# Where a level's product, its operands and the weights' remaining parts stand in the forget-gate phase

## The reference

```python
for l in range(DEPTH):
    h = rms_norm(x, norm_g[l])
    proj = h @ w_in[l]
    q_a, k_a, v_a, q_h, f_h, i_h, q_m, z = jnp.split(proj, split_points, axis=-1)
    o_a = moba_attention(partial_rope(rms_norm(q_a)), partial_rope(rms_norm(k_a)), v_a)
    o_h = rms_norm(hgrn2_chunkwise(q_h, f_h, i_h, lb_all[l]), hgrn_o_norm[l])
    o_m = memory_attention(rms_norm(q_m), km, vm)
    y = jnp.concatenate([o_a, o_h, o_m], axis=-1) * jax.nn.silu(z)
    x = x + y @ w_out[l]
# inside hgrn2_chunkwise, with lb from the layer
log_f = jnp.logaddexp(jnp.log(lb), jnp.log1p(-lb) + jax.nn.log_sigmoid(fl))
kf = (1.0 - lb) * jax.nn.sigmoid(-fl)
A = jnp.cumsum(lfc, axis=2)
decay = jnp.exp(jnp.where(causal[:, :, None], A[:, :, :, None, :] - A[:, :, None, :, :], -jnp.inf))
scores = jnp.einsum('bhtd,bhtsd,bhsd->bhts', qc, decay, kc)
```

## Time and profile before

| | |
|---|---|
| median of 3 runs | 1388.79 us |
| the profiled execution's own time | 1389.63 us |
| its span | 1387.8 us |
| TensorE matmul busy | 1349.3 us (97%) |
| VectorE busy | 971.3 us (70%) |
| ScalarE busy | 742.3 us (53%) |
| mean granted TensorE clock | 0.997 |

### The profile page before, as it was taken

One profiled execution on the slowest core, in us unless ns is written; L12 is line 12 of the kernel. 1 busy time (PEld: TensorE's weight loads), 2 busy tenths in 40 slices (PEclk: granted clock), 3 DMA queues, 4 the chain that ended last, 5 costly groups with the idle time before them and its releaser, 6 DMA issues.

```text
span 1387.8 us, 17865 instructions
## 1 busy us (share of the span) xinstructions
PE 1349.3 (97%) x7119; PEld 1146.4 (83%) x7119; DVE 971.3 (70%) x1230; ACT 742.3 (53%) x1045; POOL 57.0 (4%) x46
## 2 busy tenths in 40 slices
PE   7999999989999999999999999999999999999998
PEld 6978888978887898887877888879888887788886
DVE  6689776699776498747876555457796678565644
ACT  6864766764684565544454444346744444454432
POOL 1002000001100001000000000000100000000000
PEclk9999999999999999999999999999999999999999
DMA  8554335544343655434445554455643344476553
GB/s 294 186 169 155 100 122 182 183 129 155 113 144 131 224 176 174 147 126 144 152 152 182 182 182 168 166 180 185 200 157 123 120 143 146 145 221 186 189 180 110
DMA packets 139697, 226.25 MB, mean 163 GB/s; under 512 B 8096, under 2 KB 54880, under 8 KB 139488
## 3 DMA queue, kind: packets, MB, share of 16 engines
q1 hardware_dynamic: 137952, 222.49, 48.8%
q10 hardware_dynamic: 1664, 2.63, 0.5%
HBM read 224.05 MB, written 1.05 MB: 162 GB/s over the span
## 4 chain that ended last, share of the span: by engine, by line
PE 80%; DVE 12%; ACT 4%; issue 2%; POOL 1%; DMA 0%; SPq 0%; ACTq 0%; DVEq 0%
PE gp L613 61%; PE gp L602 7%; PE mp L585 4%; DVE arena L1466 4%; DVE wt_rest L1472 3%; PE mp L896 2%; PE mp L715 1%; DVE arena L1472 1%; PE mp L782 1%; DVE arena L1956 1%; POOL rs_out L2222 1%; DVE arena L1469 1%; PE mp L757 1%; ACT arena L1048 1%; PE mp L743 0%
## 5 line engine op out<-in xcount | busy, mean ns | idle before, releaser
L1472 DVE TENSOR_TENSOR wt_rest<-wt,wt_hi 128x1024 fp32r<-128x1024 f32 x156 | 184.1, 1221 | 77.6 <-ACT wt_hi L1080 76.9
L1080 ACT ACTIVATE wt_hi<-wt 128x1024 fp32r<-128x1024 f32 x156 | 156.8, 1054 | 101.9 <-DMA wt<-in_ffn_up 51.0
L1080 ACT ACTIVATE mix_hi<-wt 128x1024 fp32r<-128x1024 f32 x136 | 139.7, 1062 | 103.3 <-PE gp L613 58.4
L1472 DVE TENSOR_TENSOR wt_rest<-wt,mix_hi 128x1024 fp32r<-128x1024 f32 x136 | 160.5, 1220 | 34.2 <-ACT mix_hi L1080 33.3
L613 PE MATMUL gp<-wt_rest,mix_hT_hi 128*128 128x512 f32 x384 | 149.8, 390 | 0.0
L613 PE MATMUL gp<-mix_hi,mix_hT_hi 128*128 128x512 f32 x352 | 140.7, 400 | 4.6 <-DVE wt_rest L1472 3.7
L613 PE MATMUL gp<-wt_hi,hT_hi 128*128 128x512 f32 x352 | 140.2, 398 | 4.8 <-DVE wt_rest L1472 4.0
L613 PE MATMUL gp<-wt_hi,hT_rest 128*128 128x512 f32 x352 | 137.5, 391 | 0.0
L613 PE MATMUL gp<-mix_hi,mix_hT_rest 128*128 128x512 f32 x352 | 137.3, 390 | 0.0
L613 PE MATMUL gp<-wt_rest,hT_hi 128*128 128x512 f32 x352 | 137.2, 390 | 0.0
L1080 ACT ACTIVATE first_hi<-wt 128x1024 fp32r<-128x1024 f32 x104 | 106.4, 1061 | 49.1 <-PE gp L613 36.7
(11 more groups left out here) (331 smaller groups left out, 2913.7 us busy)
## 6 DMA issues: line engine op xcount, KB each, us to landing
wt<-in_w_in SPq DMA_DIRECT2D x100, 1024.0 KB, 5.0
wt<-in_ffn_gate SPq DMA_DIRECT2D x44, 512.0 KB, 4.0
wt<-in_ffn_up SPq DMA_DIRECT2D x44, 512.0 KB, 5.0
wt<-in_w_out SPq DMA_DIRECT2D x20, 1024.0 KB, 5.0
wt<-in_ffn_down SPq DMA_DIRECT2D x20, 1024.0 KB, 5.1
wt<-in_w_mem_kv SPq DMA_DIRECT2D x8, 1024.0 KB, 6.2
wt<-in_w_branch_pool SPq DMA_DIRECT2D x4, 1024.0 KB, 5.1
wt<-in_w_branch_ret SPq DMA_DIRECT2D x4, 1024.0 KB, 5.0
```

The lines of the kernel that those rows point to most:

```text
L1080: nc.scalar.activation(rounded_part(u)[:, k:k + nk, :], wt[:, u % SLOTS, k:k + nk, :], ACT.Copy)\
L1472: return nc.vector.tensor_tensor(o, i0, i1, ALU.subtract)
```

## The change

TensorE does a level's product between the two parts of a unit instead of between two units: level n after 10+n.a (before: after unit 9 + n). Level 7 and the two diagonals with level 8 part: level 7 stands between 17.a and 17.b, the diagonals and level 8 behind unit 17. The transposes `qmT` go between 18.a and 18.b. ScalarE rounds unit 10 + n ahead of `level_exp(n)` instead of behind it, unit 11 ahead of `level_exp(1)`. VectorE makes rests 10 ahead of the product with the bound and of the sum, and from there on runs one unit earlier against the levels: `diff(n)`, the rest of 10+n.a, `collect(n - 2)`, `products(n)`, the rest of 10+n.b. At n = 8 both parts of unit 18 stand behind `products(8)`; the `rests_until(18)` behind `collect(8)` finds them done. No instruction is added or removed.

```diff
--- before.py
+++ after.py
@@ -791,17 +791,20 @@
                 def y_taken(j):
                     for t in range(TT):
                         pe.wait_ge(*read_out(s(f"yT{2 * j + t}")))
-                for n, g in enumerate(("QM", "QM", "QA", "QA", "KA", "KA", "VA")):
-                    split_units(s(g), 1)
-                    hg_level(n + 1)
-                    if n == 1:
+                def level_and_values(n):
+                    hg_level(n)
+                    if n == 2:
                         flip_values()
+
+                def query_transposes():
+                    for t in range(TT):
+                        transposes(s(f"qmT{t}"), [reg("A", "QM")[:, t, P * j:P * j + P] for j in range(4)], (sig("qm_normed"), l + 1))
+                split_units(s("QM"), 1)
+                for n, g in enumerate(("QM", "QA", "QA", "KA", "KA", "VA", "VA")):
+                    split_units(s(g), 1, halfway=lambda: level_and_values(n + 1))
                 hg_diagonals()
                 hg_level(8)
-                split_units(s("VA"), 1)
-                for t in range(TT):
-                    transposes(s(f"qmT{t}"), [reg("A", "QM")[:, t, P * j:P * j + P] for j in range(4)], (sig("qm_normed"), l + 1))
-                split_units(s("Z2"), 1)
+                split_units(s("Z2"), 1, halfway=query_transposes)
                 mem_scores()
                 split_units(s("Z2"), 1)
                 mem_transposes()
@@ -1198,11 +1201,11 @@
                     nc.scalar.activation(dtmp, dtmp, ACT.Ln, bias=1.0).then_inc(sig("hg_lb_ln"), 1)
                 round_until(10)
                 move(s("IH"))
+                round_until(11)
                 level_exp(1)
-                round_until(11)
                 for n, g in ((2, None), (3, "QM"), (4, None), (5, "QA"), (6, None), (7, "KA"), (8, None)):
+                    round_until(10 + n)
                     level_exp(n)
-                    round_until(10 + n)
                     if n == 3:
                         evacuate("ihr", reg("A", "IH")[:, 1, :], bank(s("ihr")))
                     if g is not None:
@@ -1675,6 +1678,8 @@
                 rests_until(9)
                 if l > 0:
                     v(nc.vector.tensor_tensor(etmp, etmp, lbs[:, 0:4][:, :, None].to_broadcast([P, NH, S]), ALU.max))
+                rests_until(10)
+                if l > 0:
                     v(mul(ks, ks, lbs[:, 8:12][:, :, None].to_broadcast([P, NH, S])))
                 if l > 0:
                     dve.wait_ge(sig("hg_lb_ln"), l)
@@ -1777,18 +1782,23 @@
                                                                 gated_hi[j][:, t].bitcast(F), ALU.mult, ALU.subtract), st)
                         else:
                             evac(sub(gated_rest[j][:, t], bank(st, 4, P), gated_hi[j][:, t].bitcast(F)), st)
+                def first_half_rests(i):
+                    weight_rests(parts_until(first_unit(s("KM")) + i - 1) + 1)
                 diff(1)
-                rests_until(10)
+                first_half_rests(11)
                 products(1)
+                rests_until(11)
                 v(copy(ks_back, ks[:, :, S - 1:P - 1:-1]))
                 if l == 0:
                     dve.wait_ge(loaded["flips"], 16)
                 for n in range(2, 9):
                     diff(n)
-                    rests_until(9 + n)
+                    if n < 8:
+                        first_half_rests(10 + n)
                     if n > 2:
                         collect(n - 2)
                     products(n)
+                    rests_until(10 + n)
                 dve.wait_ge(sig("qm_squared"), l + 1)
                 qm = heads(reg("A", "QM"))
                 v(nc.vector.tensor_reduce(small[:, 420:428], qm_sq, X, ALU.add))
```

## The result

The change makes the kernel slightly slower: the median is 1390.99 us in 17 runs (1388.53 to 1391.89) against 1388.93 us in 17 runs of the kernel before (1385.79 to 1390.26). The ratio is 1.0016 with the interval 1.0009 to 1.0023, that is +2.06 us where -0.40 was forecast. The time lies in the forecast's range and within the 0.2% named there, but the sign is wrong and the interval leaves "no change" out. The profiled execution took 1390.78 us, its span is 1389.0.

What follows compares the result with a forecast made beforehand. TensorE, busy 97% of the span, was taken as the bound, so only its waits could be gained. Fronts -1.96 and -4.64 plus tails 2 x 3.10 gave -0.40 us: 1388.4 against the median; own range 1387.0 to 1390.0, 8-in-10 range 1382.0 to 1392.6.

Steps and rivals of the forecast that it cites:

- Layer 0, front: TensorE's wait at unit 11, ahead of level 1 in layer 0, would go: -1.96 us, with 0.4 us of room.
- Layer 1, front, -4.64: Wait and clock fall at unit 10 would go (6.37 us); a 1.73 us wait would be left at 11.a.
- The tail, +3.10 a layer: VectorE's list up to the rotation would end late, so TensorE waits at unit 19 and the `qaT` transposes, each layer.
- U: The end of unit 16, where level 7 starts in the kernel before (119.56 in layer 0); tail times count from it.
- Full clock in the tail: The forecast took the clock to stay full through the new waits at unit 19 and `qaT`: no cost counted.
- rival 1: Clock falls in a wait at `qaT`: once +3.4 us, 1391.8 (chance 0.25); in both layers 1395.2 (0.07).
- The sum: Both fronts and both tails together: -1.96 - 4.64 + 2 x 3.10 = -0.40 us.
- No wait under 3 us in this trace shows it: Argument against rival 1: in the profile before, no TensorE wait under 3 us showed a fall of the clock.
- a granted clock under 1.00 in either tail: A sign named beforehand that would show the forecast wrong: the clock below full in the tail of either layer.
- the clock in front: At unit 10 of layer 1, 2.67 us lost to half clock would be won back, as the clock stays full.
- Rival 2: The tail holds no new wait, so the front's whole gain stays: -6.6 us, 1382.2; chance 0.18.
- Rival 3: Front's wait only moves from unit 10 to 11 with its clock fall: the 4.64 us are missing, 1393.0; chance 0.05.

Runs made afterwards that it cites:

- the exponentials between: Changed kernel, with the exponentials of levels 2 to 8 between the roundings of the two parts of unit 10 + n: 1390.44 us.

## Why the prediction went wrong, step by step

Three places of TensorE's timeline mark the stretches: the first unit of weights, a unit at the start of layer 1, and the attention's values at the end of layer 1. Before, and then after:

```profile
12.25 0.79 PE L613 MATMUL gp<-first_hi,mem_hi 128*128 128x512 f32 x1 [3.13 <-DVE wt_rest L1472]
...
275.97 0.50 PE L613 MATMUL gp<-first_hi,first_hT_hi 128*128 128x512 f32 x1 [0.75 <-DVE wt_rest L1472]
...
390.87 0.49 PE L735 MATMUL mp<-arena 128*128 128x128 f32 x2 [0.41 <-DVE gated_rest L1472]
```

```profile
11.76 0.79 PE L613 MATMUL gp<-first_hi,mem_hi 128*128 128x512 f32 x1 [3.13 <-DVE wt_rest L1475]
...
276.90 0.50 PE L613 MATMUL gp<-first_hi,first_hT_hi 128*128 128x512 f32 x1 [0.74 <-DVE wt_rest L1475]
...
392.22 0.49 PE L735 MATMUL mp<-arena 128*128 128x128 f32 x2 [0.41 <-DVE gated_rest L1475]
```

- **Layer 0, front:** right. The wait at unit 11 is gone and unit 12 has none.
- **Layer 1, front, -4.64:** right in the profiled pair. From the second mark to the half unit behind level 1 (11.b now, 11.a before, so 2.73 us of work are added there): 296.88 + 2.73 - 275.97 = 23.64 us before, and 296.03 - 276.90 = 19.13 after, so -4.51. The new wait at 11.a was worked out as 1.56 us and is 1.50.
- **The tail, +3.10 a layer:** right in kind, nearly in size. With U = 117.16 the products of level 8 start at U + 2.46 (2.40 was worked out), rests 18 at U + 3.92 (3.85), the sum of KA at U + 14.61 (14.49) without idle time before it, and the rotation is there at U + 29.17 (29.05). TensorE goes on at U + 29.31 (29.14), which is 3.27 behind the U + 26.04 of before. In layer 1 it is 3.26: from the place behind level 1 to `qaT` 61.47 us before, 64.73 after.
- **Full clock in the tail, in the sum and against rival 1: this is the step that failed.** The sum has no term for it, and it measures 1.7 us in the profiled execution and 1.8 in the median. "No wait under 3 us in this trace shows it" was true and proved nothing: behind its first 6 us that trace has no wait of TensorE between 1.71 and 3.13 us, where the two new ones lie. After 2.08 us of idle in layer 1 the clock was at half for 3.4 us, which is also the sign "a granted clock under 1.00 in either tail" that the prediction named. The price in that layer was 1.7 us and not 3.4, as half clock lasted 3.4 us and not 6.8. The trace agrees in layer 1 with the rule of the Trainium skill (TensorE: Matmul & The Clock Gate, the HAM clock gate) that I set against the change, that the clock goes by how busy the array has been; layer 0, with the same pair of waits, kept 1.00.
- **The sum.** In the profiled pair, from the first mark to the third, the change costs 380.46 - 378.62 = 1.84 us. Against -0.40 that is 2.24 more: 1.7 for the clock, 2 x 0.17 for the tails, 0.13 for the front, 2.2 together. Behind the third mark the two executions take the same time to the end of their spans, 996.9 us before and 996.8 after, so nothing of the change is hidden there.
- **Over many executions: the clock in front, the second term that was off.** The forecast of -0.40 is +2.27 us for the waits (-1.96 - 1.97 + 6.20) and -2.67 for the clock in front. The runs with filled waits measure the same two parts in medians: the waits are +1.84, and the clock costs the change 1.80 and the kernel before 1.43, so it brings +0.37 and not -2.67. Nearly the whole miss is the clock's: 1.8 us in the tail, put at nothing, and 1.2 us in front, where 2.67 was read from one execution. With 1.2 to 1.7 us to either side of each part, the split is surer in its direction than in its figures. In which executions the clock falls is not explained.

Rival 2, a free tail, fell with the waits; the run with two products less, in which 0.36 us of wait is left in each layer, shows that it was worth about 6.9 us. Rival 3 fell as well. Rival 1 came halfway: its place and its cause were right, in one layer of the profiled execution and at half the price.

## What to carry to other kernels

Before work is moved half a step on one engine, read how late its last consumer may be: here a room of 0.24 us at the end of VectorE's list turned 6.5 us gained in front (1.96 + 4.51 in the sum and the profiled pair) into a small loss, and a version that gives that list room, with other edits beside it, gains 7.4. A wait of 2 us can cost nearly twice its length if the clock falls behind it (2.08 + 1.7 us in layer 1), so a sum that moves waits needs the clock on both sides, from several executions and not from one. Filling a wait with idle matmuls is a good measurement of what the clock takes, if the filler ends before the wait does.

## What the runs showed of the hardware

- The granted clock fell behind four of six waits of 2.03 to 2.08 us of TensorE (layer 1 of the change, layer 1 changed alone, both layers with the exponentials between) and stayed at 1.00 behind the other two (layer 0 of the change, layer 0 changed alone). No fall stood behind the 24 idle times of 1.49 to 1.74 us in the 13 profiled executions, their first 6 us left out.
- Half clock lasted 3.4 us in the tails, and in front 6.8 us behind 3.54 us of idle; but behind 3.50 us in the kernel with layer 0 alone changed only 3.4 (289.6 to 293.0).
- Executions of one kernel differ in this, and the spread of the times fits that: 1385.8 to 1390.7 for the kernel before, 1386.7 to 1388.2 with its wait filled, 1387.1 to 1391.8 with the exponentials between, but only 1386.8 to 1388.0 for the latter with its waits filled. The fastest executions of the kernel before lie below all of those with its wait filled, so a filler doesn't give back the best case.
- At the start TensorE runs at half speed in all 13 profiled executions, behind 3.1 to 3.3 us of idle, but the granted clock of the views shows it in six of them only (from 11 to 14 us of the kernel before with its wait filled, a stretch at 0.78). In the others the view reads 1.00 there, while equal matmuls start 0.43 us apart; in the kernel before it is 0.43 up to 16.7 us and 0.23 from 17.0 on:

```profile
11.00:14.00 3.00, 2.06 (x6) 1.67 (x7) 3.00 (x4) 3.00 (x5) 0.00 (x0) 0.78 1.05 388
```

```profile
15.82 0.63 PE L613 MATMUL gp<-first_hi,mem_rest 128*128 128x512 f32 x1
16.25 0.63 PE L613 MATMUL gp<-first_hi,mem_hi 128*128 128x512 f32 x1
...
17.22 0.39 PE L613 MATMUL gp<-first_hi,mem_hi 128*128 128x512 f32 x1
17.45 0.39 PE L613 MATMUL gp<-wt_rest,mem_hi 128*128 128x512 f32 x1
```

So at the start the distance between equal matmuls is the thing to read. The mean granted clock of an execution is no guide either: of the kernel before with its wait filled, the executions that read 0.997 took 1387.5 us on average and those that read 0.999 took 1387.6.
